# Placing the operands of 272-column matmuls modulo 256 bytes: lower parts of tokens and weights moved, higher weights by slot

## The reference

```
block 1, twice:  x += 0.5 * norm(ffn(norm(x)))       ffn(x) = (silu(x Wg) * (x Wu)) Wd, inner width 2816
                 x += norm(attention(norm(x)))       first neighbourhood attention, then differential attention
                 x += 0.5 * norm(ffn(norm(x)))       the last of these needs only the 256 real tokens
block 2, once:   z = norm(x) W_in                    then RWKV-7 and mLSTM mixers, gates, W_out
                 x += PEER(norm(x))                  128*128 single-neuron experts, 8 heads, top 16
                 final norm
```

## Time and profile before

| what | value |
|---|---|
| median of three runs | 2215.82 us |
| the profiled execution's own time | 2213.92 us |
| its span, first to last instruction | 2212.1 us |
| TensorE's matmul records, busy | 2168.7 us, 98% |
| weight loads, busy | 2058.4 us, 93% |
| VectorE, busy | 1631.9 us, 74% |
| ScalarE, busy | 1043.0 us, 47% |
| DMA | 163 GB/s mean |

### The profile page before, as it was taken

How to read it: one execution, slowest core, us unless ns; L and a number is a source line. 1 busy time by engine, 2 the same in 40 slices (tenths; PEclk the granted TensorE clock), 3 DMA queues, 4 the chain that set the end, 5 groups by cost and what they waited for, 6 DMA issues and landing times. The chain is left out here.

```text
span 2212.1 us, 46147 instructions
## 1 busy us (share of the span) xinstructions
PE 2168.7 (98%) x18208; PEld 2058.4 (93%) x18208; DVE 1631.9 (74%) x3097; ACT 1043.0 (47%) x1695; POOL 106.0 (5%) x46
## 2 busy tenths in 40 slices
PE   9999999999999999999899999999999999999998
PEld 9999989999999998999889989999999999888887
DVE  6665868765875687876686587699899966777776
ACT  5444555443544466544453345444444444333333
POOL 0000000000000000000000000198000000000000
PEclk9999999999999999999999999999999999999999
DMA  6563535554556443556332226455344455555554
GB/s 217 179 197 128 195 110 175 177 199 145 168 175 201 133 169 130 172 193 218 116 125 69 79 94 203 164 181 189 125 144 145 147 170 197 190 190 190 190 190 152
DMA packets 100061, 361.11 MB, mean 163 GB/s; under 512 B 11544, under 2 KB 15784, under 8 KB 99760
## 3 DMA queue, kind: packets, MB, share of 16 engines
q1 hardware_dynamic: 99888, 358.65, 49.5%
HBM read 357.55 MB, written 1.05 MB: 162 GB/s over the span
## 5 line engine op out<-in xcount | busy, mean ns | idle before, releaser
L1144 DVE TENSOR_TENSOR w_lo<-ring,w_hi 128x1024 fp32r<-128x1024 f32 (+1 forms) x301 | 393.0, 1307 | 187.6 <-ACT w_hi L893 187.0
L893 ACT ACTIVATE w_hi<-ring 128x1024 fp32r<-128x1024 f32 (+1 forms) x301 | 337.5, 1126 | 339.5 <-PE ps L524 326.5
L524 PE MATMUL ps<-x_hi,w_hi 128*128 128x272 f32 (+1 forms) x1608 | 462.7, 288 | 2.0 <-DVE x_lo L1214 1.5
L524 PE MATMUL ps<-x_lo,w_hi 128*128 128x272 f32 (+1 forms) x1608 | 460.1, 286 | 0.0
L524 PE MATMUL ps<-x_hi,w_lo 128*128 128x272 f32 (+1 forms) x1608 | 458.3, 285 | 0.0
L524 PEld LDWEIGHTS ps<-x_hi,w_hi 128*128 128x128 f32 x1608 | 301.8, 188 | 5.0 <-ACT x_hi L934 1.7
L524 PEld LDWEIGHTS ps<-x_lo,w_hi 128*128 128x128 f32 x1608 | 302.6, 188 | 0.2
L524 PEld LDWEIGHTS ps<-x_hi,w_lo 128*128 128x128 f32 x1608 | 302.3, 188 | 0.0
L3315 ACT ACTIVATE v_gated_hi<-ring 128x1024 fp32r<-128x1024 f32 x128 | 136.0, 1062 | 213.7 <-PE ps L3362 213.7
L3105 PE MATMUL ps<-tok_hi,u_mid_hi 128*128 128x256 f32 x704 | 201.8, 287 | 0.6 <-POOL u_mid_lo L263 0.6
L3362 PE MATMUL ps<-v_gated_hi,gated_gelu_hi 128*128 128x512 f32 x512 | 202.3, 395 | 0.0
(11 more groups left out here) (522 smaller groups left out, 5059.0 us busy)
## 6 DMA issues: line engine op xcount, KB each, us to landing
ring<-in_gate_up SPq DMA_DIRECT2D x173, 512.0 KB, 3.5
ring<-in_peer_v SPq DMA_DIRECT2D x128, 512.0 KB, 3.3
ring<-in_down SPq DMA_DIRECT2D x64, 704.0 KB, 4.1
ring<-in_peer_u_mid SPq DMA_DIRECT2D x88, 512.0 KB, 3.3
ring<-in_w_in SPq DMA_DIRECT2D x46, 512.0 KB, 3.4
ring<-in_peer_u_early SPq DMA_DIRECT2D x40, 512.0 KB, 3.3
ring<-in_project SPq DMA_DIRECT2D x32, 512.0 KB, 4.1
ring<-in_da_qk SPq DMA_DIRECT2D x18, 512.0 KB, 4.3
```

The costliest lines, as they stand in the source:

```text
L524: mm = nc.tensor.matmul(ps[:, bank, 0:ntok], parts[left][:, slot, t * P:(t + 1) * P], rhs[right][:, k, 0:ntok], start=start and n == 0, st ...
L893: A.activation(parts[0][:, n % SLOTS, 0:width[n]], ring[:, n % SLOTS, 0:width[n]], ACT.Copy).then_inc(hi_done.sem, 1)
L1144: V.tensor_tensor(parts[1][:, n % SLOTS, 0:width[n]], ring[:, n % SLOTS, 0:width[n]], parts[0][:, n % SLOTS, 0:width[n]].bitcast(F32), ALU ...
```

## The change

Places modulo 256, measured from the tokens' higher part as above:

| | before | after, 272-column stages | after, 256-column stages |
|---|---|---|---|
| `x_lo`, `o_lo` | 0 | 192 | 0 |
| `hidden_lo` | 0 | 128 | 0 |
| `w_hi`, slots 0, 1, 2, 3 | 64 in all | 64, 128, 192, 0 | 64 in all |
| `w_lo` | 192 | 128 | 192 |

Each of these tiles is allocated some columns longer, and two views are cut from it: one shifted (or, for `w_hi`, with a pitch longer by 16 columns) for stages before `da_o`, one as before for the later ones. `queries_item`, which has 256 columns, belongs to the first kind. In the last stage, measured from `v_at`, where the moving `v_gated` lies, `gated_gelu_hi` goes from 0 to 192 and `gated_gelu_lo` from 0 to 64. Tiles allocated behind the longer ones move by up to a few hundred bytes. No instruction, wait or semaphore is added, removed or reordered.

```diff
-TOKENS_AT = {"hi": 128, "lo": 128 + 0}
-WEIGHTS_AT = {"hi": (128 + 64) % LINE, "lo": (128 + 192) % LINE}
-LO_SLOT = SLOT_COLS + 0
+TOKENS_AT = 128
+WEIGHTS_AT = {"hi": 128 + LEAD["hi"], "lo": 128 + LEAD["lo"] - LINE}
+WIDE_ON = {"w_hi": 4 * 64 // 4, "w_lo": 192 // 4, "x": 192 // 4, "o": 192 // 4, "hidden": 128 // 4}
...
+        def two_views(name, tile, on, inner):
+
+            later = tile[:, 0:tile.shape[1] - on].rearrange("p (s c) -> p s c", c=inner)
+            return tile[:, on:tile.shape[1]].rearrange("p (s c) -> p s c", c=inner), later
+
+        def weights_tile(name):
+            on = WIDE_ON[name]
+            if name == "w_hi":
+                tile = sb_in(ctx, name, [P, SLOTS * SLOT_COLS + on], F32R)
+                return tile[:, :].rearrange("p (s c) -> p s c", c=SLOT_COLS + on // SLOTS), tile[:, 0:SLOTS * SLOT_COLS].rearrange("p (s c) -> p s c", c=SLOT_COLS)
+            return two_views(name, sb_in(ctx, name, [P, SLOTS * SLOT_COLS + on], F32R), on, SLOT_COLS)
+
+        def tokens_tile(name, part, rows):
+            on = WIDE_ON[name] if part == "lo" else 0
+            at_phase(ctx, f"before_{name}_{part}", TOKENS_AT)
+            return two_views(name, sb_in(ctx, f"{name}_{part}", [P, rows * TOKEN_PITCH + on], F32R), on, TOKEN_PITCH)
...
+        def parts_of(n):
+
+            late = n >= first["da_o"]
+            return w_hi[late], w_lo[late]
+
+        def x_of(b):
+            return [views[b == 5] for views in x_views]
+
+        def o_of(i):
+            return [views[i == 1] for views in o_views]
+
+        def hidden_of(n):
+            return [views[n == 3] for views in hidden_views]
...
-            def products(slot, t, k, bank, ntok, rhs, start, stop):
+            def products(item, t, k, bank, ntok, rhs, start, stop):
+                parts = parts_of(item)
                 for n, (left, right) in enumerate(TERMS):
-                    mm = nc.tensor.matmul(ps[:, bank, 0:ntok], parts[left][:, slot, t * P:(t + 1) * P], rhs[right][:, k, 0:ntok],
+                    mm = nc.tensor.matmul(ps[:, bank, 0:ntok], parts[left][:, item % SLOTS, t * P:(t + 1) * P], rhs[right][:, k, 0:ntok],
                                           start=start and n == 0, stop=stop and n == 2)
                 return mm
...
-            at_phase(c, "before_gated_gelu", v_at)
-            gated_gelu = [sb_in(c, f"gated_gelu_{part}", [P, 2, SEQ], F32R) for part in ("hi", "lo")]
+            gated_gelu = []
+            for part in ("hi", "lo"):
+                at_phase(c, f"before_gated_gelu_{part}", v_at - LEAD[part])
+                gated_gelu.append(sb_in(c, f"gated_gelu_{part}", [P, 2, SEQ], F32R))
```

More of the change, by code:

```diff
@@ L360, in first_block @@
         assert nc.sbuf_base == base + W_HI_AT
-        parts = [sb_in(ctx, "w_hi", [P, SLOTS, SLOT_COLS], F32R)]
+        def two_views(name, tile, on, inner):
[11 more added lines that the diff above has]
+            return two_views(name, sb_in(ctx, f"{name}_{part}", [P, rows * TOKEN_PITCH + on], F32R), on, TOKEN_PITCH)
+        w_hi = weights_tile("w_hi")
         sb_in(ctx, "inv_space", [P, T])
         spare = sb_in(ctx, "spare", [P, (W_IN_PARTS_AT - (nc.sbuf_base - base)) // 4])
[L364 to L367, removed]
+        x_views = [tokens_tile("x", part, KD) for part in ("hi", "lo")]
         h = sb_in(ctx, "h_first", [P, KD, 2 * (P + META)])
@@ L370, in first_block @@
         at_phase(ctx, "before_w_lo", WEIGHTS_AT["lo"])
-        parts.append(sb_in(ctx, "w_lo", [P, SLOTS, LO_SLOT], F32R))
+        w_lo = weights_tile("w_lo")
         sq = sb_in(ctx, "sq", [P, KD, T])
@@ L401, in first_block @@
         at = region
-        hidden, spots = [], {}
+        hidden_views, spots = [], {}
         for part in ("hi", "lo"):
-            at += (TOKENS_AT[part] - at) % LINE
-            hidden.append(nc.alloc_sbuf_tensor_at(f"hidden_{part}", [P, KF, TOKEN_PITCH], F32R, offset=at))
-            at += 4 * KF * TOKEN_PITCH
+            at += (TOKENS_AT - at) % LINE
+            on = WIDE_ON["hidden"] if part == "lo" else 0
+            tile = nc.alloc_sbuf_tensor_at(f"hidden_{part}", [P, KF * TOKEN_PITCH + on], F32R, offset=at)
+            hidden_views.append(two_views("hidden", tile, on, TOKEN_PITCH))
+            at += 4 * (KF * TOKEN_PITCH + on)
         for name in ("gated", "silu", "upped", "product"):
@@ L585, in ffn @@
                 ntok = tokens_of(n)
+                x, hidden = x_of(b), hidden_of(n)
                 n0, taken0 = first[f"gate_up_{n}"], taken_before[f"gate_up_{n}"]
@@ L611, in ffn @@
                         for left in range(2):
-                            nc.tensor.matmul(ps[:, m, 0:ntok], parts[left][:, (n0 + m) % SLOTS, k * P:(k + 1) * P], x[0][:, k, 0:ntok],
+                            nc.tensor.matmul(ps[:, m, 0:ntok], parts_of(n0 + m)[left][:, (n0 + m) % SLOTS, k * P:(k + 1) * P], x[0][:, k, 0:ntok],
                                              start=(k == 0 and left == 0), stop=False)
@@ L635, in ffn @@
                             pe.wait_ge(hidden_lo, KF * n + k + 1)
-                        mm = products((n0 + i) % SLOTS, t, k, 4 + m % 2, ntok, hidden, k == 0, k == KF - 1)
+                        mm = products(n0 + i, t, k, 4 + m % 2, ntok, hidden, k == 0, k == KF - 1)
                     mm.then_inc(used, 1)
@@ L650, in attention @@
                         for left in range(2):
-                            nc.tensor.matmul(ps[:, m, 0:T], parts[left][:, (n0 + m) % SLOTS, k * P:(k + 1) * P], x[0][:, k, 0:T],
+                            nc.tensor.matmul(ps[:, m, 0:T], parts_of(n0 + m)[left][:, (n0 + m) % SLOTS, k * P:(k + 1) * P], x[0][:, k, 0:T],
                                              start=(k == 0 and left == 0), stop=False)
@@ L654, in attention @@
                     for m in range(3):
-                        mm = nc.tensor.matmul(ps[:, m, 0:T], parts[0][:, (n0 + m) % SLOTS, k * P:(k + 1) * P], x[1][:, k, 0:T],
+                        mm = nc.tensor.matmul(ps[:, m, 0:T], parts_of(n0 + m)[0][:, (n0 + m) % SLOTS, k * P:(k + 1) * P], x[1][:, k, 0:T],
                                               start=False, stop=(k == KD - 1))
@@ L1574 @@
 W_HI_AT = KD * T * 4 + 128
-LAST_INV_AT = W_HI_AT + SLOTS * SLOT_COLS * 4
+LAST_INV_AT = W_HI_AT + (SLOTS * SLOT_COLS + WIDE_ON["w_hi"]) * 4
 EARLY_ROWS = 5
```

33 lines of the change are left out of this document (19 added, 14 removed).

## The result

The changed kernel is slower. Its median is 2221.98 us (8 runs, 2220.56 to 2223.81) against 2214.59 us for the kernel before (8 runs, 2213.01 to 2218.29): ratio 1.0035, 95% interval 1.0026 to 1.0043. I had forecast 2201 us, so the sign is wrong and the range just missed the median. The profiled execution took 2221.5 us with a span of 2219.7 us; the span before was 2212.1 us, so it grew by 7.6 us.

The account below looks back on a forecast made before the run. TensorE's matmul distances were taken to bound the kernel; -15.0 - 0.3 - 0.6 + 1.0 = -14.9 us took the span from 2212.1 to 2197.2 us, hence a median of 2201 us, range 2189 to 2220 us.

Parts of the forecast that it names:

- What bounds the kernel: Whole kernel: TensorE almost everywhere, so time is the number of matmuls by the distance between their starts.
- Distances by length: Matmul loops: 124.4 ns for 272 columns, 113.3 for 256, 226.7 for 512; 7.08 ns per group of 16 columns.
- So one rate fits: 256- and 512-column matmuls fit 7.08 ns per group exactly; 272 columns and the queries pay some 4 ns on top.
- What the 4 ns may be: 272-column matmuls: 4.0 ns charged to reading the same 64-byte place twice running, once per matmul; queries 4.5 ns.
- part 1: 272-column triples: lower tokens moved, 373.3 to 365.3 ns each, 1872 triples, 15.0 us saved.
- repeats: Handovers where one row ends on the 64-byte place where the next begins, 4.0 ns each; two of three per triple relieved.
- Only the mean fits: Prediction's own objection: distances within a 272-column triple are uneven, so equal repeat costs match only their mean.
- Parts 2 and 3: Interleaved starts of stages, 0.3 us saved, and queries' 64 triples, 0.6 us saved.
- Part 4: New places of higher and lower weights: taken as 0, bounds +22.5 and -7.5 us.
- Part 5: Last stage's shifted tiles: taken as 0, bounds -7.7 and +6.1 us, inner distance already 226.7 ns.
- Part 6: Attentions: of 3.3 us gained there, 1.0 us turns into waits for VectorE.
- The new leads are worse: Rival, 0.20: next weights' load meets the moving walk on the same 64-byte place; +12 us net, 2228 us.

Follow-up runs that it names:

- lower tokens alone: Kernel before with only `x_lo` and `o_lo` moved to 192 and `hidden_lo` to 128, weights and last stage as before: 2220.23 us, ratio 1.0033.
- 288, 304 and 320 columns: Kernel before with gate and up of ffn 0, 1 and 2 reading that many columns, the added ones zeros with unused results: 2256.29 us, run once.
- Lower weights at 128 alone: Kernel before with only `w_lo` of the 272-column stages moved from 192 to 128, last stage as before: 2224.35 us, ratio 1.0051.
- (0, 64, 64): `x_lo`, `w_hi`, `w_lo` places: kernel before with `w_lo` at 64, 2217.45 us; with `w_lo` first at 128 in items 0 to 7 of ffn 1 and 2, 2207.87 us.
- the whole map: Three kernels with weights' places varied by groups of items, `x_lo` by ffn, last stage by slot: 2222.04, 2217.22 and 2221.71 us against 2212.74 us before.

## Why the prediction was wrong

- *What bounds the kernel.* Right: TensorE's distances decide, the clock and the counts did not move, and the span followed the distances.
- *Distances by length.* The distances were read rightly, and 7.08 ns per group fits 256 and 512. "So one rate fits" was then carried to 272 as if 17 groups were a floor. No steady loop came below 370 ns per triple. Nor was 226.7 ns the rate of the last stage: it was read from the last six distances of one item, and over all items of the kernel before the mean inside an item is 230.0 ns, since the first matmuls of an item stand further apart.
- *What the 4 ns may be, and part 1 (-15.0 us).* This is the step that failed. "A row of 272 columns ... ends on the very place on which the next row begins" was true and not the cause: with two of three repeats gone, lower tokens alone gave 380.0 ns in gate and up and 373.3 in `down` instead of 365.3, and 288, 304 and 320 columns, which repeat nothing, pay too. In its place the runs showed a distance that hangs on the combination of the tiles' places and on what ran just before, between 370.0 and 380.0 ns per triple. The evidence against stood in the prediction's own next lines: three unequal distances in a triple (122.5, 126.7 and 124.2 ns over ffn 1) cannot be three equal repeats. "Only the mean fits" should have cut the step's weight, since one mean fits any rule with one free price.
- *Parts 2 and 3 (-0.9 us).* The interleaved starts sum to 39.8 us in both traces, and the queries went from 23.8 to 24.0 us: no gain.
- *Part 4 (0, bounds +22.5 and -7.5).* Wrong value, honest bounds. "Three of four leads are shown to cost nothing" took leads shown at 256 and 512 columns over to 272. Lower weights at 128 alone took the triple to 380.0 ns and the median to +10.7 us.
- *Part 5 (0, bounds -7.7 and +6.1).* Wrong value: +3.5 us, inside the bounds. An item went from 2759.9 to 2787.5 ns, and the later matmuls of an item, 227 ns apart before, are 229 to 234 ns apart. "A stage whose inner rate has no room" excludes only a gain, and rested on the 226.7 ns of one item; I had put it at the middle all the same.
- *Part 6 (+1.0).* The attentions gave nothing back, since there was nothing to give.
- *The rivals.* "The new leads are worse" won. Its direction holds. Its price of 2.3 ns per matmul, 6.9 per triple, is reached only by the worst slot of gate and up (373.3 to between 377.0 and 379.9 ns) and not by `down` (about 1 ns per triple), so that +12 us net exceeds the +7.4 us found; and its mechanism, a meeting on the same place, isn't shown: (0, 64, 64) puts `w_lo` one place on from `x_hi` and is the best cell by one entrance and among the worst by another.

What stays open: why so many patterns fit sixteens of clocks, and by what state the entrance chooses. The runs show that both happen, not how. What sets the last stage's item also stays open.

## What to carry to other kernels

A rule for operand placement taken from means over a loop is not worth a forecast with a sign; put the placements in one kernel as groups of a few items and read the distance of each. Then run the best cell as a whole kernel, in every stage in which it is to hold, since a cell measured behind one neighbour may fall into another pattern behind the next (370 and 380 ns here). Check first how far any cell lies from the present one: here the whole map spans 370 to 380 ns, with 373.3 in hand, so some 6 us were to be had and 12 to be lost.

## What was unexpected of the hardware

- With 272 columns, the places of four tiles modulo 256 bytes move the distance of matmuls between 123.3 and 126.7 ns, most often in steps of 3.33 ns per triple, at a granted clock of 1.00 throughout. The Trainium skill, "TensorE: Matmul & The Clock Gate", "Back-to-back issue gap", gives its formula of columns over 2.4 GHz plus 2.5 ns for what it calls the isolated gap and measured figures for sustained streams, neither with a term for places; these rows do not agree with a distance that depends on columns alone.
- The same instructions at the same places ran at 370.0 or 380.0 ns per triple, steadily for more than 40 items, by what ran just before them; with no tile moved at all, `down` of ffn 1 and 2 ran at 373.3 or 376.7 ns.
- In the last stage, waits for the lower weights fell from 9.7 to 3.0 us (1870 to 2200 us) while the stage grew by 3.5 us: a shorter wait is no sign of a faster stage, since the distances between matmuls can take more than it gives.
